# A four-layer NSA/FoX decoder trunk: the second compression matrix loaded in four pieces, and FoX opened with four units by tile

## What is computed

```
def nsa_mixer(h, w_in, cmp_pe, cmp_w1, cmp_b1, cmp_w2, w_out, rel_bias):
    q, kc, vc, ks, vs, kw, vw, gates = jnp.split(h @ w_in, splits, axis=-1)
...
    def compress(a, pe, w1, b1, w2):
        blocks = a[:, :, blk_idx] + pe
        flat = blocks.reshape(B, G, nc, CMP_BLOCK * dh)
        return jax.nn.gelu(flat @ w1 + b1) @ w2

    k_cmp = compress(kc, cmp_pe[0], cmp_w1[0], cmp_b1[0], cmp_w2[0])
    v_cmp = compress(vc, cmp_pe[1], cmp_w1[1], cmp_b1[1], cmp_w2[1])
...
def fox_mixer(h, w_in, b_f, w_out):
    q, k, v, f_logit = jnp.split(h @ w_in, [Q_DIM, 2 * Q_DIM, 3 * Q_DIM], axis=-1)
    log_f = jax.nn.log_sigmoid((f_logit + b_f).astype(jnp.float32))
    cum = jnp.cumsum(log_f, axis=1).transpose(0, 2, 1)
...
```

## Time and profile before

| | |
|---|---|
| median of 3 runs | 1026.38 us (1026.32 to 1027.04) |
| profiled execution, its own time | 1028.11 us |
| its span in the trace | 1026.3 us, granted clock 0.997 |
| TensorE busy | 1011.2 us, 99% of the span |
| HBM read | 185.99 MB |

### The profile page before, as it was taken

The page is one execution under the profiler, slowest core; times in us unless marked ns, Lnnn a source line. Parts: engine busy times, 40 slices in busy tenths (PEclk is TensorE's granted clock), DMA queues, the critical chain, the costliest instruction groups (busy, mean ns, idle before and its releaser), DMA issues.

```text
span 1026.3 us, 14374 instructions
## 1 busy us (share of the span) xinstructions
PE 1011.2 (99%) x5979; PEld 867.0 (84%) x5979; DVE 641.2 (62%) x777; ACT 518.9 (51%) x712; POOL 109.3 (11%) x210
## 2 busy tenths in 40 slices
PE   8999999998999999999999999999999999999997
PEld 7888888897756898888889888888988689888886
DVE  5756555746696765656576655556648776655654
ACT  5544544644465554444565454445546565454442
POOL 0000000312153300000020000001103320000000
PEclk9999999999999999999999999999999999999999
DMA  9757765578203265655556555655675336655551
GB/s 268 250 203 256 237 221 203 164 225 276 94 1 110 97 219 192 202 175 196 194 175 209 202 188 181 204 180 189 206 248 166 120 104 206 204 178 192 204 173 75
DMA packets 138376, 189.58 MB, mean 185 GB/s; under 512 B 7394, under 2 KB 120391, under 8 KB 138312
## 3 DMA queue, kind: packets, MB, share of 16 engines
q1 hardware_dynamic: 133734, 172.83, 50.8%
q0 software_dynamic: 4432, 15.77, 4.5%
q10 hardware_dynamic: 146, 0.07, 0.0%
HBM read 185.99 MB, written 1.09 MB: 182 GB/s over the span
## 4 chain that ended last, share of the span: by engine, by line
PE 91%; DVE 3%; POOL 2%; DMA 1%; ACT 1%; issue 1%; DVEq 0%; POOLq 0%; ACTq 0%
PE ps L1182 88%; PE ps L1572 1%; PE ps L1384 1%; DMA raw<-in_nsa_w_in 1%; POOL ms L417 1%; POOL rstd L419 1%; DVE normed L830 1%; ACT work L546 1%; DVE probT_buf L951 1%; DVE normed L925 1%; POOL ms_half L413 0%; DVE res L814 0%; DMA res<-in_x 0%; DVE work L925 0%; DVE wlo L781 0%
## 5 line engine op out<-in xcount | busy, mean ns | idle before, releaser
L773 DVE TENSOR_TENSOR wlo<-raw,whi 128x2048 fp32r<-128x2048 f32 x145 | 332.7, 2294 | 134.1 <-ACT whi L520 133.9
L1182 PE MATMUL ps<-xhl,whi 128*128 128x512 f32 (+1 forms) x1664 | 389.0, 377 | 0.0
L1182 PEld LDWEIGHTS ps<-xhl,whi 128*128 128x128 f32 x1664 | 288.1, 190 | 50.1 <-issue 2.8
L520 ACT ACTIVATE whi<-raw 128x2048 fp32r<-128x2048 f32 x150 | 286.3, 1909 | 33.1 <-DMA raw<-in_ffn_w_up 9.5
L1182 PEld LDWEIGHTS ps<-xhl,wlo 128*128 128x128 f32 x1536 | 208.1, 191 | 13.9
L1182 PE MATMUL ps<-xhl,wlo 128*128 128x256 f32 x1536 | 213.2, 282 | 0.0
L1182 PE MATMUL ps<-whi,xhl 128*128 128x256 f32 (+1 forms) x640 | 133.6, 318 | 0.0
L1182 PE MATMUL ps<-whi,hhi 128*128 128x512 f32 x320 | 124.9, 390 | 0.0
L1182 PE MATMUL ps<-wlo,hhi 128*128 128x512 f32 x320 | 124.9, 390 | 0.0
L1182 PE MATMUL ps<-whi,hlo 128*128 128x512 f32 x320 | 124.5, 389 | 0.0
L1182 PEld LDWEIGHTS ps<-whi,xhl 128*128 128x128 f32 x640 | 101.5, 191 | 9.6 <-issue 2.6
(11 more groups left out here) (174 smaller groups left out, 770.8 us busy)
## 6 DMA issues: line engine op xcount, KB each, us to landing
raw<-in_ffn_w_down SPq DMA_DIRECT2D x44, 1024.0 KB, 4.8
raw<-in_ffn_w_gate SPq DMA_DIRECT2D x40, 1024.0 KB, 5.2
raw<-in_ffn_w_up SPq DMA_DIRECT2D x40, 1024.0 KB, 5.2
raw<-in_fox_w_in SPq DMA_DIRECT2D x10, 1024.0 KB, 5.4
raw<-in_nsa_w_in SPq DMA_DIRECT2D x8, 1024.0 KB, 5.3
raw<-in_nsa_w_out SPq DMA_DIRECT2D x4, 1024.0 KB, 5.3
raw<-in_fox_w_out SPq DMA_DIRECT2D x4, 1024.0 KB, 4.8
g_post<-in_norm_g POOLq DMA_DIRECT2D x6, 512.0 KB, 4.0
```

The lines of the kernel that those rows point to most:

```text
L520: nc.scalar.activation(whi[:, u % RING, :], raw_of(u), ACT.Copy).then_inc(w_hi, 1)
L773: nc.vector.tensor_tensor(wlo[:, u % RING, :], raw_of(u), whi[:, u % RING, :].bitcast(F32), ALU.subtract).then_inc(w_lo, 1)
L1182: return nc.tensor.matmul(out_, l, r, start=start, stop=stop)
```

## The change

The second compression matrix is loaded in four DMAs of 512 KB where there was one of 2 MB. The first keeps the place of the old one. The second waits until unit `U0[1]+6` is done, the third for `U0[1]+7`, the fourth for `U0[1]+8` (the counter is one above the unit's number). The third and fourth stand ahead of the four `kX` DMAs in GpSimd's program.

In FoX the opening now takes in the fourth unit, as in the other sublayers: new functions `tokens_high` and `tokens_low` put all high products of a tile first, and the low products of units `u0+2` and `u0+3` after both tiles. `hi(u0+3)` moves ahead of ScalarE's `split_x` of tile 1, and `lo_part(u0+2, 1)` behind VectorE's. The gate products follow the fourth unit where they preceded it.

```diff
+            def load_w1(kv, b):
+                pool.dma_start(w1[:, 4 * b:4 * b + 4, :],
+                               cmp_w1[0, kv][512 * b:512 * b + 512, :].rearrange("(k p) n -> p k n", p=P)).then_inc(w1_in[kv], 16)
...
             pair_tokens(0)
             pair_tokens(1)
             pool.wait_ge(part_mm, 1)
-            pool.dma_start(w1, cmp_w1[0, 1].rearrange("(k p) n -> p k n", p=P)).then_inc(w1_in[1], 16)
-
+            load_w1(1, 0)
             nc.gpsimd.memset(probT_buf[:, 0:1024], 0.0).then_inc(hidR_zero, 1)
+            pool.wait_ge(unit_done, U0[1] + 7)
+            load_w1(1, 1)
 
             pool.wait_ge(flat_ready, 2)
             nc.gpsimd.memset(pairs[:, :], 0.0).then_inc(probc_zero, 1)
+            for b in range(2, 4):
+                pool.wait_ge(unit_done, U0[1] + 6 + b)
+                load_w1(1, b)
             for r in range(2):
                 pool.wait_ge(proj_ready, 7 + r)
                 for a in range(2):
...
                         if by_token(kind, k):
+                            if kind == "fox" and k == 0:
+                                act.wait_ge(w_lo, u0 + 3)
...
-                    if kind == "fox":
-                        hi(u0 + 3)
...
-                    if KINDS[s + 1] != "fox":
-                        hi(u + 3)
+                    hi(u + 3)
                     split_x(s + 1, 1)
...
-                    if KINDS[s + 1] == "fox":
-                        lo_part(u + 2, 1)
-                        split_x(s + 1, 1)
-                    else:
-                        split_x(s + 1, 1)
-                        lo_part(u + 2, 1)
+                    split_x(s + 1, 1)
+                    lo_part(u + 2, 1)
...
+            def tokens_high(u, bank, t, before={}):
+                wh = wcols(u % RING)[0]
+                tile = slice(t * P, (t + 1) * P)
+                n = 0
+                pe.wait_ge(w_hi, u + 1)
+                for k in range(KT):
+                    for v in (xhi, xlo):
+                        if n in before:
+                            before[n]()
+                        mm(ps[:, bank, t * UC:(t + 1) * UC], v[:, k, tile], wh[:, k, :], t == 0 and n == 0, False)
+                        n += 1
+
+            def tokens_low(u, bank):
+                pe.wait_ge(w_lo, u + 1)
+                wl = wcols(u % RING)[1]
+                for t in range(TT):
+                    for k in range(KT):
+                        last = mm(ps[:, bank, t * UC:(t + 1) * UC], xhi[:, k, t * P:(t + 1) * P], wl[:, k, :], False, t == TT - 1 and k == KT - 1)
+                last.then_inc(unit_done, 1)
...
-                high = twin_high if feature else tokens_tile
+                high, low = (twin_high, twin_low) if feature else (tokens_high, tokens_low)
+                fourth = YB if feature else OB + 1
                 tokens(u0, u0 % RING, GB, (0,), 4 * s)
                 tokens_tile(u0 + 1, UB, 0)
                 high(u0 + 2, OB, 0, {12: T1[0], 15: T1[1]})
-                if feature:
-                    twin_high(u0 + 3, YB, 0)
+                high(u0 + 3, fourth, 0)
                 tokens(u0, u0 % RING, GB, (1,), 4 * s + 2)
                 tokens(u0 + 1, (u0 + 1) % RING, UB, (1,))
                 high(u0 + 2, OB, 1)
...
-                pe.wait_ge(w1_in[kv], 16 if kv else 64)
+                pe.wait_ge(w1_in[kv], 64)
...
-                    for k in range(2, nproj - 3):
-                        if k >= 3:
+                    for k in range(3, nproj - 3):
+                        if k >= 4:
                             project(k)
-                        if k == 2:
+                        if k == 3:
                             gates(YB, 48, GWC)
```

More of the change, by code:

```diff
@@ L460, in _ @@
                 pool.wait_ge(unit_done, 17 + 2 * b)
-                pool.dma_start(w1[:, 4 * b:4 * b + 4, :],
-                               cmp_w1[0, 0][512 * b:512 * b + 512, :].rearrange("(k p) n -> p k n", p=P)).then_inc(w1_in[0], 16)
+                load_w1(0, b)
             between_sublayers(0)
@@ L1422, in open_sublayer @@
                 high(u0 + 2, OB, 1)
[L1423 to L1428, removed]
+                if product_T:
+                    product_T()
+                low(u0 + 2, OB)
+                high(u0 + 3, fourth, 1)
+                low(u0 + 3, fourth)
             def setup():
```

## The result

The changed kernel takes 1034.69 us (median of 6 runs, 1033.92 to 1035.88) against 1026.76 us before (6 runs, 1026.32 to 1027.58): ratio 1.0077, 95% interval 1.0067 to 1.0086. It is 7.9 us slower. The forecast was slower by 3.9 us, 1030.3 us, and its range ended at 1032.4: right in sign and place, short by half in size.

The account below looks back on a forecast made before the run. TensorE, busy 99% of the span, was taken as the bound, so only its gaps count. -4.45 (`kcmp` wait and clock) - 0.47 (FoX) + 7.2 (copy stall) + 1.6 (clock) = +3.9, median 1030.3 us, range 1026.9 to 1032.4.

Parts of the forecast that it names:

- The `kcmp` gap: TensorE's wait for `kcmp`, due to unit `u0+9` landing late: a gap of 2.87 us that the change would remove.
- The 1.58 us for the slow clock behind it: TensorE's half clock after the `kcmp` wait: a half unit took 4.47 us against 2.89; forecast as gained back.
- The copies behind the pieces: Before `scores(0)`: `kX` copies queued on GpSimd behind the fourth piece would stall TensorE 7.2 us, from 258.5 to 265.7.
- That is 5.5 us, close to the loaded end of the row. I take that: Landing time of the second `kX` copy, issued at 260.2, landing near 265.7; from 1.83 MB at 336 GB/s.
- costs nothing more: The second pair of `kX` copies, issued 1.04 us later and needed one `scores(0)` later, was charged no time.
- The row's 5.7 us: Longest time of the four `kX` copies in the profile before, 2.2 to 5.7 us, taken as bounding the new copies.
- the same 1.6 us, and 2.0 at most: TensorE's half clock after the new stall before `scores(0)`: charged 1.6 us, upper bound 2.0.
- FoX: TensorE's wait for `wlo` near 727 us would go, -0.47 us, with the later gates hidden by 2.0 us of cover.
- Quick copies: Rival, chance 0.16: `kX` copies land quickly, stall before `scores(0)` only 3.9 us, total 1027.0 us.
- The longer stall: Rival, chance 0.12: piece and copies strictly in turn, 8.4 us stall before `scores(0)`, clock cost 2.0: 1031.9 us.
- The rival of a late `u0+9`: Rival, chance 0.02: the pieces do not bring unit `u0+9` early, so the 4.45 us gain falls away: 1034.7 us.
- The rule of the Trainium skill: DMA priced at 2.0 us plus bytes at 436 GB/s: `kX` copies land at 262.5, total near 1027.1 us.

Follow-up runs that it names:

- fox_only: The changed kernel with only its FoX half, the second matrix in one DMA as before: 1026.10 us against 1026.91, ratio 0.9992.
- second_pair_held: The changed kernel, but GpSimd waits for the first pair of key copies to land before issuing the second: 1036.92 us, ratio 1.0102.
- pieces_only: The kernel before with only the four matrix pieces put in for its one DMA, FoX as before: 1035.46 us, ratio 1.0081.
- copies_alone: The changed kernel with the fourth piece released by unit 7 and unit 12's load held back one unit, copies still waiting for unit 8: 1029.55 us, ratio 1.0030.
- keys_alone_late: The changed kernel with the fourth piece released by unit 7 beside the third, key copies still held until unit 8: 1033.16 us, ratio 1.0059.

## Why the prediction was wrong in size

- **The `kcmp` gap goes: right.** Unit 9's load took 5.6 us, the wait left the list, `compressed_scores(0)` began at 252.54 with no gap.
- **The 1.58 us for the slow clock behind it: right for the profiled execution, wrong for the median, as far as the runs tell.** In fox_only's trace it is not paid, and 46 of 65 executions of the kernel before show a higher mean clock and, but for one, a shorter time. I took one execution's price for the kernel's. This part of the error, the smaller one, lay on the gain side and made the forecast too low by about 1.6 us.
- **The copies behind the pieces: right in place, order and moment.** The fourth piece was issued 0.44 us after TensorE's next work was due, the first copy 0.75 us behind it, as forecast. The list of waits is headed by `kvN<-kvN`, once.
- **"That is 5.5 us, close to the loaded end of the row. I take that": this step failed.** The copies took up to 7.5 us, and the stall was 9.29 instead of 7.2 us. The bytes were summed over unit, piece and the first pair only; the second pair "costs nothing more", but second_pair_held shows that it counts, 0.94 us of the gap. The rate was taken from a stretch of loads, 336 GB/s, while the last 2 us of the gap, with the copies still to finish, moved 186 GB/s; the remaining 1.15 us of the stall are put down to this, which is argued and not tested. The row's 5.7 us, from before, was no like case: at 248 the matrix had landed (247.65), and about 1.05 MB of units moved ahead of those copies, where now 1.05 MB of unit and 0.52 MB of piece did. And its 2.2 us, "with a unit load in flight", had only the last 0.3 MB of that unit ahead.
- **The clock after the new stall, "the same 1.6 us, and 2.0 at most": too small** for the profiled execution, 2.89 us. pieces_only, with the same stall, paid 1.53. With the stall so nearly the same, its length does not set the cost, and my upper bound was no bound. The median's own cost is not traced; 7.93 + 2.87 + 0.48 - 9.29 leaves 2.0 us for it.
- **FoX: right**, 0.48 us for 0.47. The gates' path had cover, and the list shows no new wait.
- **The rivals.** Quick copies did not come: 6.9 us was the least. The longer stall was the case that happened, in its place and with more than its price: piece and copies did move behind the unit, but the piece landed after 7.8 us, not 7.2 at most, and the second copy 1.0 us behind it. The rival of a late `u0+9` gave 1034.7 us, the measured time by chance: its mechanism did not happen, unit 9 came early. The rule of the Trainium skill that was weighed (DMA: Bandwidth & Descriptors, the anatomy of one DMA by the gpsimd path), 2.3 us for such a copy, agrees with the second pair of second_pair_held, 2.2 and 2.5 us, nearly with copies_alone, 2.6 to 2.7, and not with the copies that had a unit or a piece issued shortly ahead of them, 4.4 to 8.6 us.

Against the medians: -2.87 - 0.48 + 9.29, and between 1.5 and 2.9 for the clock, is +7.4 to +8.8; measured +7.9.

## What to carry to other kernels

A wait put into an in-order queue delays everything behind it: before a load is moved to a later signal, look which short transfer stands next in that queue, and when its reader wants it. In these runs a small copy landed about when the larger transfers issued shortly ahead of it had landed, whichever queue they were in. So price it with all the bytes issued ahead of it and about it, not by itself, and hold back the transfer that has long slack (unit 11 here). One rate does not fit: with 0.52, 1.05, 1.57 and 2.10 MB issued about the copies, their own included, they took 2.7, 4.6, 6.1 and 7.1 us. Price the slow clock after a gap from several executions, not from the one that was profiled.

## What was not expected of the hardware

- Copies of 128 KB within the chip's memory beside the engines took 2.2 and 2.5 us as a pair with nothing else in flight, four of them 2.7 us each almost alone, 4.6 behind a piece of 512 KB, 6.1 beside a unit of 1 MB, 7.1 with both, and 6.2 on another engine's queue beside a unit and a piece.
- Loads and copies of different queues moved mostly in the order of their issue and were not shared out: in the changed kernel only the unit's queue moved from 260 to 263 us, 0.85 MB, with a piece and four copies issued on the other. No experiment was made to test this order by itself.
- While mostly such copies were in flight, the core moved 186 GB/s at a DMA share of 0.81, against 352 GB/s at 1.12 with loads. That copies are the slower kind was not measured by itself.
- After gaps of 2.4 to 9.4 us the slow clock cost 0 (2.40 us, fox_only), 1.58 (2.87, before), 1.82 (3.77, copies_alone), 1.69 (7.20, keys_alone_late), 2.89 (9.29, changed) and 1.53 us (9.37, pieces_only), one execution each. Its cost did not follow the length of the gap.
